# Both feed-forward blocks of a fused two-block transformer kernel computed by Strassen's seven products instead of eight

## The chip, the cores and the metric

The kernel runs on one core of a Trainium2 chip. The metric is the device time of one launch in microseconds (us). A core has TensorE (PE in the profile, PEld for its weight loads), VectorE (DVE), ScalarE (ACT), GpSimd (POOL) and SyncE (SP, which issues most of the transfers).

## The reference, cut to what matters

One sequence of 1024 tokens with 1024 features goes through a first transformer block (a SwiGLU feed-forward block, a token mixer, a second feed-forward block) and then through a two-layer second model. The change is in the two feed-forward blocks (FFN) of the first block:

```
def rms_norm(x, g):
    xf = x.astype(jnp.float32)
    y = xf * lax.rsqrt(jnp.mean(xf * xf, axis=-1, keepdims=True) + RMS_EPS)
    return (y * g.astype(jnp.float32)).astype(x.dtype)

def swiglu(x, w_gate, w_up, w_down):
    return (jax.nn.silu(x @ w_gate) * (x @ w_up)) @ w_down
...
        f1 = swiglu(rms_norm(x, ffn1_pre_g[l]), ffn1_w_gate[l], ffn1_w_up[l], ffn1_w_down[l])
        x = x + FFN_RESIDUAL_WEIGHT * rms_norm(f1, ffn1_post_g[l])
        m = token_mixer(rms_norm(x, mix_pre_g[l]), ...)
        x = x + rms_norm(m, mix_post_g[l])
        f2 = swiglu(rms_norm(x, ffn2_pre_g[l]), ffn2_w_gate[l], ffn2_w_up[l], ffn2_w_down[l])
        x = x + FFN_RESIDUAL_WEIGHT * rms_norm(f2, ffn2_post_g[l])
```

w_gate and w_up are 1024 x 2816, w_down is 2816 x 1024, all float32.

## The kernel before, in words

Everything is kept feature-major: 128 features on the partitions, tokens along the row, in two halves of 512 tokens (`HALVES`, c = 0 and 1). A float32 product is made of three matmuls in fp32r: each operand is split into a high part (a ScalarE copy) and a low part (value minus high part), and `pe_product` adds high x high (L401), weight low x high (L402) and weight high x low (L403), for each 128-row piece k.

Weights come in units of 128x1024 (512 KB), in the order of the list `UNITS`. SyncE loads them into two `raw` tiles, `act_units` makes `whi` (L366), `pool_units` makes `wlo` on GpSimd (L375), in a ring of three. One FFN has 22 column tiles j of 128 columns. For each j and each half c TensorE makes a gate product and an up product, 8 pieces k x 3 = 24 matmuls of 512 columns each, so 96 matmuls for a j. VectorE scales both by the norm's factor (`dve_scaled`, L794), ScalarE takes silu (L775), VectorE multiplies (L820), ScalarE and GpSimd make the high and the low part `hh`, `hl` (L781, L845). These stay in SBUF in a ring of four j. After every two j the down product of that pair is added: 8 feature tiles x 2 halves, each 2 pieces x 3 = 6 matmuls, and VectorE adds the PSUM result to `acc` (L831). That makes 22 x 96 + 11 x 96 = 3168 matmuls in each FFN.

Each engine runs its own list in program order, and semaphores order them against each other; there is no scheduler. `ffn_places` interleaves the work of j and of the down products on ScalarE, VectorE and GpSimd. Before an FFN stand the norms n1 (FFN 1) and n3 (FFN 2), behind it n2 and n4. Those behind it start during the last down products: the last pair's down products go through all eight tiles of half 0 first and then those of half 1, and beside the first four of half 1 TensorE sums the squares of half 0 (`after.beside`, L566), VectorE makes the root (`dve_variance` L590, `dve_root` L611 to L616), and `dve_apply` (L633, L638) begins when the last product is in.

Of the kernel before, what the change touches and what calls it, by code (L numbers as in the profile page):

```python
# [27 lines left out]
def _units():  # L28
    out = []

    def ffn(f):
        for b in range(11):
            out.extend([f"G{f}.{2 * b}", f"U{f}.{2 * b}"])
            if b:
                out.extend([f"D{f}.{b - 1}.0", f"D{f}.{b - 1}.1"])
            out.extend([f"G{f}.{2 * b + 1}", f"U{f}.{2 * b + 1}"])
        out.extend([f"D{f}.10.0", f"D{f}.10.1"])

    ffn(1)
# [4382 lines left out]
```

## Time and profile before

| what | value |
| --- | --- |
| three runs | 4032.33, 4038.79 and 4038.66 us, median 4038.66 us |
| span of the profiled execution | 4037.5 us (nothing beside its span is recorded) |
| TensorE busy | 3909.1 us, 97% |
| VectorE, ScalarE, GpSimd busy | 1910.4 us (47%), 1388.5 us (34%), 1425.1 us (35%) |
| share of the chain that ended last | PE 79%, DVE 12%, ACT 4%, POOL 3% |
| transfers | 206.07 MB, mean 51 GB/s |

Busy time of an engine is the union of its instructions' times. The matmuls of a group overlap each other, so a group's sum of durations is more than the time that it takes. FFN 1 lies at about 15 to 766 us of the span and FFN 2 at about 1550 to 2295 us.

### The profile page before, as it was taken

How to read it: one execution, taken by the hardware profiler on the slowest of the kernel's cores; microseconds unless marked ns; L12 is line 12 of the kernel's file. 1: busy time of each engine (PE TensorE's matmuls, PEld its weight loads, DVE VectorE, ACT ScalarE, POOL GpSimd, SP SyncE). 2: the span in 40 equal slices, each digit the busy share in tenths (PEclk: the TensorE clock that was granted, in tenths of full speed). 3: DMA queues.
4: the chain of work that ended last, by engine and by line, in shares of the span. 5: the costliest groups of instructions: out<-in, count | busy, mean ns of one | idle time of the engine just before them, and what ended most of it. 6: DMA issues, size and time to landing. Idle time of an engine off the chain costs nothing.

```text
span 4037.5 us, 49424 instructions
## 1 busy us (share of the span) xinstructions
PE 3909.1 (97%) x20636; PEld 3176.7 (79%) x20636; DVE 1910.4 (47%) x2824; ACT 1388.5 (34%) x2239; POOL 1425.1 (35%) x858
## 2 busy tenths in 40 slices
PE   8999999999999899999999999999999999999998
PEld 6888888666665467888888789999968998888877
DVE  3323222644355626323232477654377436666664
ACT  3111111322222234111111354331283336666663
POOL 2322323233543452223222224432271233434364
PEclk9999999999999999999999999999999999999989
DMA  2111111110000021111111101121112210000014
GB/s 95 52 42 53 44 51 51 55 58 22 27 22 16 16 95 53 53 47 47 47 51 44 42 27 43 53 95 54 64 50 74 106 58 24 27 29 29 24 64 139
DMA packets 57854, 206.07 MB, mean 51 GB/s; under 512 B 7392, under 2 KB 11008, under 8 KB 57248
## 3 DMA queue, kind: packets, MB, share of 16 engines
q1 hardware_dynamic: 45744, 158.55, 11.9%
q0 software_dynamic: 9328, 41.75, 2.8%
q8 instruction: 163, 2.67, 0.3%
q10 hardware_dynamic: 2560, 2.61, 0.2%
q14 instruction: 59, 0.48, 0.0%
HBM read 177.40 MB, written 25.49 MB: 50 GB/s over the span
## 4 chain that ended last, share of the span: by engine, by line
PE 79%; DVE 12%; ACT 4%; POOL 3%; issue 1%; DMA 0%; ACTq 0%; DVEq 0%; POOLq 0%
PE ps L401 16%; PE ps L403 15%; PE ps L402 15%; PE ps L3674 4%; PE ps L3606 2%; PE ps L3608 2%; PE ps L3607 2%; PE ps L1419 2%; POOL wlo L375 2%; PE ps L1421 2%; PE ps L1420 2%; PE ps L3658 2%; PE ps L3704 2%; PE ps L566 2%; PE ps L1538 2%; PE ps L1496 1%
## 5 line engine op out<-in xcount | busy, mean ns | idle before, releaser
L375 POOL TENSOR_TENSOR wlo<-raw,whi 128x1024 fp32r<-128x1024 f32 x286 | 692.5, 2431 | 799.7 <-ACT whi L366 799.6
L401 PE MATMUL ps<-fxh,whi 128*128 128x512 f32 x1488 | 602.7, 405 | 33.0 <-DVE fxl L653 17.3
L402 PE MATMUL ps<-fxh,wlo 128*128 128x512 f32 x1488 | 580.2, 390 | 0.0
L403 PE MATMUL ps<-fxl,whi 128*128 128x512 f32 x1488 | 580.1, 390 | 0.0
L401 PE MATMUL ps<-xh,whi 128*128 128x352 f32 (+1 forms) x1400 | 473.4, 338 | 6.3 <-DVE xl L653 2.7
L366 ACT ACTIVATE whi<-raw 128x1024 fp32r<-128x1024 f32 x286 | 294.8, 1049 | 455.5 <-PE ps L403 390.2
L402 PE MATMUL ps<-xh,wlo 128*128 128x352 f32 (+1 forms) x1400 | 450.5, 322 | 0.0
L403 PE MATMUL ps<-xl,whi 128*128 128x352 f32 (+1 forms) x1400 | 450.0, 321 | 0.0
L845 POOL TENSOR_TENSOR hl<-t,hh 128x512 fp32r<-128x512 f32 x88 | 114.1, 1296 | 722.7 <-ACT hh L781 722.7
L401 PEld LDWEIGHTS ps<-fxh,whi 128*128 128x128 f32 x1488 | 280.1, 188 | 111.2 <-issue 30.0
L402 PEld LDWEIGHTS ps<-fxh,wlo 128*128 128x128 f32 x1488 | 280.0, 188 | 67.4 <-issue 11.9
L403 PEld LDWEIGHTS ps<-fxl,whi 128*128 128x128 f32 x1488 | 279.9, 188 | 58.7
L3979 POOL TENSOR_TENSOR ospl<-osp,osph 128x672 fp32r<-128x672 f32 (+4 forms) x144 | 191.1, 1327 | 357.8 <-ACT osph L3800 356.8
L831 DVE TENSOR_TENSOR acc<-acc,ps 128x512 f32<-128x512 f32 x320 | 219.9, 688 | 205.0 <-PE ps L403 205.0
L401 PEld LDWEIGHTS ps<-xh,whi 128*128 128x128 f32 x1400 | 265.2, 189 | 17.8 <-issue 5.9
L401 PE MATMUL ps<-hh,whi 128*128 128x512 f32 x704 | 276.8, 393 | 1.2 <-POOL wlo L375 1.2
L403 PE MATMUL ps<-hl,whi 128*128 128x512 f32 x704 | 274.0, 389 | 0.0
L402 PE MATMUL ps<-hh,wlo 128*128 128x512 f32 x704 | 273.9, 389 | 0.0
L402 PEld LDWEIGHTS ps<-xh,wlo 128*128 128x128 f32 x1400 | 264.5, 189 | 8.1 <-issue 2.4
L403 PEld LDWEIGHTS ps<-xl,whi 128*128 128x128 f32 x1400 | 264.1, 189 | 0.0
L794 DVE TENSOR_TENSOR t<-ps,rs 128x512 f32<-128x512 f32 x88 | 60.6, 691 | 389.8 <-PE ps L403 389.8
L781 ACT ACTIVATE hh<-t 128x512 fp32r<-128x512 f32 x88 | 55.6, 632 | 497.2 <-DVE t L820 497.2
(431 smaller groups left out, 7771.7 us busy)
## 6 DMA issues: line engine op xcount, KB each, us to landing
raw<-in_w_dram SPq DMA_DIRECT2D x286, 512.0 KB, 3.3
rs_scratch<-res POOLq DMA_DIRECT2D x2, 4160.0 KB, 15.2
res<-rs_scratch POOLq DMA_DIRECT2D x8, 520.0 KB, 5.1
szin<-zs_scratch SPq DMA_DIRECT2D x8, 520.0 KB, 3.3
gs_scratch<-oot POOLq DMA_DIRECT2D x8, 520.0 KB, 5.7
res<-rs_scratch POOLq DMA_DIRECT2D x2, 1408.0 KB, 7.5
og<-gs_scratch POOLq DMA_DIRECT2D x16, 176.0 KB, 2.6
oot<-rs_scratch POOLq DMA_DIRECT2D x4, 704.0 KB, 5.5
```

The lines of the kernel that those rows point to most:

```text
L366: act.x.activation(K.whi[n % 3][:, :], K.raw[n % 2][:, :], ACT.Copy).then_inc(*S.up("w_hi", n))
L375: pool.x.tensor_tensor(K.wlo[n % 3][:, :], K.raw[n % 2][:, :], K.whi[n % 3][:, :], ALU.subtract).then_inc(*S.up("w_lo", n))
L401: pe.x.matmul(out, wh, xh, start=k == 0, stop=False)
L402: pe.x.matmul(out, wl, xh, start=False, stop=False)
L403: last = pe.x.matmul(out, wh, xl, start=False, stop=k == K - 1)
L566: pe.x.matmul(K.bank(b, n), K.m("ones"), square_tile(K, L, first)[:, 0:n], start=begin, stop=k == 7, skip_group_check=True).then_inc(*S.up ...
L831: dve.x.tensor_tensor(acc, acc, pp, ALU.add).then_inc(*S.up("dve_acc", (f, b, ft, c)))
L845: pool.x.tensor_tensor(K.hl[:, s, c0:c1], K.t[2 * c + 1][:, :], K.hh[:, s, c0:c1], ALU.subtract).then_inc(*S.up("pool_ffn", (f, j, c)))
L1419: pe.x.matmul(K.bank(b), a, x, start=k == 0, stop=False)
L1420: pe.x.matmul(K.bank(b), b_, x, start=False, stop=False)
L3674: last = pe.x.matmul(PS[:, (4 + i) * 512 + x0:(4 + i) * 512 + x1], mat[:, :], part[n % 2][:, i, 0:x1 - x0], start=first, stop=False, skip_ ...
L3979: pool.x.tensor_tensor(K.ospl[n % 2][:, :, 0:x1 - x0], K.osp[n % 2][:, :, 0:x1 - x0], K.osph[n % 2][:, :, 0:x1 - x0], ALU.subtract).then_i ...
```

## The change

Both FFNs work on a list of steps (`STEPS`), one step being a 128x512 weight operand (256 KB) that TensorE uses for 12 matmuls of 512 columns. For j = 0 and 1 the products stay as they were ("std", 4 steps for a j, each used twice as often). For j = 2 to 21 the gate and up products of both halves are a 2x2 block product (gate and up x lower and upper 512 features x two token halves), made by Strassen's algorithm in Winograd's form: seven steps M1, M5, M6, M3, M7, M2, M4 in place of eight. The down product is made at the end, in four blocks of 3, 3, 3 and 2 pairs of 128-row pieces, again seven products for eight: 77 steps. An FFN then has 2 x 96 + 20 x 84 + 77 x 12 = 2796 matmuls.

Strassen's products need sums. Sums of weights: four of the seven weight operands (M5, M6, M3, M7), on VectorE in the gate part and on GpSimd in the down part (`raw_sum`). Sums of token rows of the gate part: made once in each FFN by VectorE (`dve_mix`), beside the std products. Sums of rows of the down part: on VectorE (`dve_row_sum`), 4 of 7 steps. Sums of products: in PSUM, where later products go on in the bank of earlier ones, and in copies on ScalarE and reads on VectorE between them (`beside`); in the down part VectorE adds 28 tiles for each block to `acc` (`total`). The silu products are written to DRAM scratch `hs` and read back as rows of the down part, and their high and low parts are made again for each step (`act_row`, `dve_row_low`). The norm tiles of n1 and n3 have places of their own, rs1 is one tile of 512 columns, and the squares of the norm behind an FFN stand in the last step of all (`after.beside(p)` for p = 0 to 3).

```
+ORDER = ("M1", "M5", "M6", "M3", "M7", "M2", "M4")
+BLOCKS = ((0, 3), (3, 6), (6, 9), (9, 11))
...
+def pool_operand(pool, f, n):
...
+    pool.wait_ge("fw_hi", (f, n))
+    pool.x.tensor_tensor(lo, raw_tile(K, step, RAW_OF[step[2]]), hi, ALU.subtract).then_inc(*S.up("fw_lo", (f, n)))
...
+def pair_bank(p, m):
+
+    return 3 * p + {"M1": 0, "M6": 0, "M7": 0, "M4": 0, "M5": 1, "M3": 1, "M2": 2}[m]
...
+    def gate(n):
+        _, j, m = STEPS[n]
+        b = pair_bank(j % 2, m)
+        wh, wl = operand(n)
+        pe.bank(b)
...
+    act_operand(act, f, 4)
+    act_operand(act, f, 5)
+    std(0, 0)
+    act_mix(act, f, (0, 0))
+    act_operand(act, f, 6)
+    act_operand(act, f, 7)
+    std(0, 1)
+    act_mix(act, f, (0, 1))
...
+    std(1, 1)
+    act_mix(act, f, (1, 1))
+    late_done(act, norms)
+    for n in range(FIRST_GATE, NSTEP):
+        act_operand(act, f, n + 4)
+        before = STEPS[n - 1]
+        if before[0] == "gate":
+            beside(before[1], before[2])
+        act_row(act, f, n + 3)
...
+    std(0, 0)
+    dve_mix(dve, f, (0, 0), pre)
+    std(0, 1)
+    dve_mix(dve, f, (0, 1), pre)
+    raw_sum(dve, f, 9)
+    std(1, 0)
+    late_done(dve, norms)
+    dve_mix(dve, f, (1, 0), pre)
+    raw_sum(dve, f, 10)
+    raw_sum(dve, f, 11)
+    std(1, 1)
+    raw_sum(dve, f, 12)
+    dve_mix(dve, f, (1, 1), pre)
+    for n in range(FIRST_GATE, NSTEP):
+        before = STEPS[n - 1]
+        if before[0] == "gate":
+            beside(before[1], before[2])
+        if n + 5 < FIRST_DOWN:
+            raw_sum(dve, f, n + 5)
+        if STEPS[n][0] == "down":
+            totals(n)
+        dve_row_low(dve, f, n + 3)
+        dve_row_sum(dve, f, n + 4)
...
+    for n in range(FIRST_GATE, NSTEP):
+        pool_operand(pool, f, n + 4)
+        if FIRST_DOWN <= n + 5 < NSTEP:
+            raw_sum(pool, f, n + 5)
```

A step's `act_operand` waits until the step six before it is used up, its `act_row` until the one four before it is. TensorE's M6 goes on in M1's PSUM bank, so it waits until ScalarE has copied M1 out of it (`u1`, L998).

The first place where the order matters is ScalarE's list in FFN 1, around the passage from j = 0 and 1 to the rest. Before, with j = 1 here as one of many (whi is the high part of a weight unit, t_76 and t_78 take silu):

```order
L366 ACTIVATE whi_58<-raw_56 128x1024
L775 ACTIVATE t_76<-t_76 128x512
L781 ACTIVATE hh<-t_77 128x512
L775 ACTIVATE t_78<-t_78 128x512
L781 ACTIVATE hh<-t_79 128x512
```

Of the change (fwh is a step's high part, u_100 takes silu of j = 1, L983 makes the high parts of the mixed rows of M4, and L998 copies M1's bank):

```order
L811 ACTIVATE fwh_77<-fpa 128x512
L811 ACTIVATE fwh_78<-fpa 128x512
L992 ACTIVATE u_100<-u_100 128x512
L983 ACTIVATE fxh<-fyl 128x512 x4
L811 ACTIVATE fwh_73<-fpa 128x512
L811 ACTIVATE fwh_74<-fpa 128x512
L998 ACTIVATE u_94<-ps 128x512
```

The copy out of M1's bank now stands behind four high parts of rows that VectorE makes in its last piece of `dve_mix`.

VectorE's list ahead of those four is this, from the scaling of j = 1's half 1 (L1053, L1055, L1117) on; the L1081 to L1087 rows are one of the four mixed rows of M4, and three more follow with the low part (L1097) of each:

```order
L1053 TENSOR_TENSOR u_100<-ps,rs_69 128x512
L1055 TENSOR_TENSOR u_101<-ps,rs_69 128x512
L1117 TENSOR_TENSOR u_101<-u_101,u_100 128x512
L792 TENSOR_TENSOR fpa<-fpa 128x512
L1081 TENSOR_TENSOR fyh<-res 128x512
L1083 TENSOR_TENSOR fyl<-res 128x512
L1084 TENSOR_SCALAR fyl<-fyl,vec 128x512
L1087 SCALAR_TENSOR_TENSOR fyl<-fyh,vec,fyl 128x512
```

None of these rows was there before except the first three, which had another form.

The second place is GpSimd's list. Before, in the steady part of an FFN (hl is the low part of a silu product, wlo that of a weight unit):

```order
L845 TENSOR_TENSOR hl<-t_77,hh 128x512
L845 TENSOR_TENSOR hl<-t_79,hh 128x512
L375 TENSOR_TENSOR wlo_63<-raw_57,whi_60 128x1024
L375 TENSOR_TENSOR wlo_61<-raw_56,whi_58 128x1024
```

Of the change, in the down part (L820 makes a step's low part, L792 the sum of weights of the step behind it):

```order
L820 TENSOR_TENSOR fwl_82<-fpb,fwh_76 128x512
L792 TENSOR_TENSOR fpb<-fpb,u_96 128x512
L820 TENSOR_TENSOR fwl_83<-fpb,fwh_77 128x512
L792 TENSOR_TENSOR u_94<-u_94,u_97 128x512
L820 TENSOR_TENSOR fwl_84<-u_94,fwh_78 128x512
L792 TENSOR_TENSOR u_95<-u_95,u_98 128x512
L820 TENSOR_TENSOR fwl_79<-u_95,fwh_73 128x512
```

Low parts and sums alternate, and between a sum and the low part that uses it lies ScalarE's high part of that sum. This holds for the 12 steps of M5, M6, M3 and M7 of a block of three; the other nine have a low part alone.

## Rows read from the trace of the kernel before

**Rows 1.** The page: span and busy times of the engines.

```profile
span 4037.5 us, 49424 instructions
PE 3909.1 (97%) x20636; PEld 3176.7 (79%) x20636; DVE 1910.4 (47%) x2824; ACT 1388.5 (34%) x2239; POOL 1425.1 (35%) x858
```

**Rows 2.** The page's groups: sum of durations, mean ns of one, idle before.

```profile
L401 PE MATMUL ps<-fxh,whi 128*128 128x512 f32 x1488 | 602.7, 405 | 33.0 <-DVE fxl L653 17.3
L401 PE MATMUL ps<-hh,whi 128*128 128x512 f32 x704 | 276.8, 393 | 1.2 <-POOL wlo L375 1.2
```

**Rows 3.** Timeline of PE in FFN 1: start, us, instruction.

```profile
239.64 0.39 PE L401 MATMUL ps<-hh,whi 128*128 128x512 f32 x1
239.87 0.39 PE L402 MATMUL ps<-hh,wlo 128*128 128x512 f32 x1
...
252.34 0.39 PE L403 MATMUL ps<-hl,whi 128*128 128x512 f32 x1
```

**Rows 4.** Waits of PE, from 55 to 766 us and from 1600 to 2300 us.

```profile
PE ps L401 <- POOL wlo L375: 7.2, 12, 0.9
...
PE ps L401 <- POOL wlo L375: 6.8, 11, 0.9
```

**Rows 5.** Groups of VectorE by form: busy us, mean ns of one, idle before.

```profile
L831 DVE TENSOR_TENSOR acc<-acc,ps 128x512 f32<-128x512 f32 x320 | 219.9, 688 | 205.0 <-PE ps L403 205.0
L820 DVE TENSOR_TENSOR t<-t,t 128x512 f32<-128x512 f32 x88 | 61.9, 703 | 9.6 <-DVE t L794 0.9
L2320 DVE TENSOR_SCALAR scv<-sxin,vec 128x1040 f32<-128x1040 f32 x12 | 9.7, 806 | 0.1
```

**Rows 6.** Groups of ScalarE and GpSimd by form, 0 to 820 us.

```profile
L781 ACT ACTIVATE hh<-t 128x512 fp32r<-128x512 f32 x44 | 27.8, 632 | 248.6 <-DVE t L820 248.6
...
L845 POOL TENSOR_TENSOR hl<-t,hh 128x512 fp32r<-128x512 f32 x44 | 57.1, 1297 | 361.3 <-ACT hh L781 361.3
```

**Rows 7.** Timeline behind FFN 1, GpSimd's rows, then VectorE's rows.

```profile
742.94 4.76 POOL L375 TENSOR_TENSOR wlo<-raw,whi 128x1024 fp32r<-128x1024 f32 x2
764.21 2.98 POOL L581 TENSOR_TENSOR t<-t,t 128x512 f32<-128x512 f32 x2 [8.18 <-ACT t L546]
...
744.83 0.69 DVE L831 TENSOR_TENSOR acc<-acc,ps 128x512 f32<-128x512 f32 x1 [0.67 <-PE ps L403]
764.37 1.68 DVE L611 TENSOR_TENSOR t<-t,t 128x512 f32<-128x512 f32 x1
766.08 1.65 DVE L613 SCALAR_TENSOR_TENSOR t<-t,t 128x512 f32<-128x512 f32 x1
768.37 1.28 DVE L831 TENSOR_TENSOR acc<-acc,ps 128x512 f32<-128x512 f32 x2
```

**Rows 8.** Timeline at the start of FFN 1, VectorE and ScalarE.

```profile
49.51 0.69 DVE L590 TENSOR_SCALAR t<-ps 128x512 f32<-128x512 f32 x1 [4.29 <-PE ps L566]
77.38 0.42 DVE L794 TENSOR_TENSOR t<-ps,rs1a 128x256 f32<-128x256 f32 x1 [4.68 <-PE ps L403]
...
53.45 1.28 ACT L775 ACT_TABLE_LOAD   x1
```

**Rows 9.** Timeline at the end of FFN 1 and of FFN 2.

```profile
766.28 2.08 PE L566 MATMUL ps<-t,mat 128*128 128x512 f32 x4
...
769.57 0.94 DVE L633 SCALAR_TENSOR_TENSOR acc<-acc,vec,t 128x512 f32<-128x512 f32 x1
...
2295.06 4.89 PE L566 MATMUL ps<-lq,mat 128*128 128x352 f32 x16
...
2295.86 0.56 DVE L633 SCALAR_TENSOR_TENSOR acc<-acc,vec,t 128x336 f32<-128x336 f32 x1
```

**Rows 10.** Windows: busy PE, PEld, DVE, ACT, POOL, then clock, DMA share, GB/s.

```profile
776.00:780.00 4.00, 3.02 (x6) 1.46 (x5) 3.96 (x7) 2.46 (x4) 0.00 (x0) 0.52 0.20 81
780.00:784.00 4.00, 4.00 (x10) 2.27 (x9) 3.93 (x7) 3.04 (x6) 0.00 (x0) 0.62 0.00 0
```

**Rows 11.** Transfers by line (KB each, us to landing), and a window at the start.

```profile
raw<-in_w_dram SPq DMA_DIRECT2D x286, 512.0 KB, 3.3
...
12.00:16.00 4.00, 1.27 (x3) 0.83 (x3) 1.79 (x2) 3.52 (x8) 4.00 (x2) 1.00 1.04 394
```

More of the change, by code:

```diff
@@ L29, in _units @@
     out = []
[L31 to L39, printed above, removed]
     out.append("IN.24")
@@ new lines, in _ffn_steps @@
+def _ffn_steps():
+    out = []
+    for j in range(STD):
+        out.extend(("std", j, q) for q in ("A11", "A12", "A21", "A22"))
+    for j in range(STD, 22):
+        out.extend(("gate", j, m) for m in ORDER)
+    for b, (k0, k1) in enumerate(BLOCKS):
+        for m in ORDER:
+            out.extend(("down", b, m, k) for k in range(k1 - k0))
+    return out
+STEPS = _ffn_steps()
+STEP_AT = {s: n for n, s in enumerate(STEPS)}
+NSTEP = len(STEPS)
+FIRST_GATE = 4 * STD
+FIRST_DOWN = FIRST_GATE + 7 * (22 - STD)
@@ new lines, in down @@
+    def down(n):
+        _, b, m, k = STEPS[n]
+        end = k == BLOCKS[b][1] - BLOCKS[b][0] - 1
+        wh, wl = operand(n)
+        pe.wait_ge("ft_lo", (f, n))
+        xh, xl = row_ring(K, n)
+        for p in range(4):
+            o, pb = 128 * p, (0 if m in ("M1", "M6", "M7", "M4") else 4) + p
+            if k == 0:
+                pe.bank(pb)
+            pe.x.matmul(K.bank(pb), wh[:, o:o + 128], xh, start=m in FRESH and k == 0, stop=False, skip_group_check=True)
+            pe.x.matmul(K.bank(pb), wl[:, o:o + 128], xh, start=False, stop=False, skip_group_check=True)
+            last = pe.x.matmul(K.bank(pb), wh[:, o:o + 128], xl, start=False, stop=end, skip_group_check=True)
+            if p == 3:
+                last.then_inc(*S.up("pe_step", (f, n)))
+            elif end:
+                last.then_inc(*S.up("pe_step", (f, n, p)))
+            if end:
+                pe.banks[pb] = [("dve_acc", (f, b, m, p))]
+            if n == NSTEP - 1:
+                after.beside(p)
+        S.steps[f, n] = "pe_step", (f, n)
@@ L783, in act_ffn, with std, copied @@
-    ffn_places(act, f, gate_up, lambda b, c, ft: None, act_units, after)
+    def std(j, c):
+        ea = K.u[4 * (j % 2) + 2 * c][:, :]
+        act.wait_ge("dve_fe", (f, j, "gs", c))
+        act.x.activation(ea, ea, ACT.Silu).then_inc(*S.up("act_fe", (f, j, "silu", c)))
+    def copied(j, m, what, tile, free):
+        for name, key in free:
+            act.wait_ge(name, key)
+        act.wait_ge("pe_step", (f, STEP_AT["gate", j, m]))
+        act.x.activation(tile, K.bank(pair_bank(j % 2, m)), ACT.Copy).then_inc(*S.up("act_fe", (f, j, what)))
@@ L786, in dve_scaled @@
+    after.end()
 def dve_scaled(dve, f, j, c, norms):
     S, K = dve.S, dve.K
[L790 to L795 removed]
+    tile = (K.rs0, K.rs1)[c][:, :]
     b = 2 * ((2 * j + c) % 2)
+    u = 4 * (j % 2) + 2 * c
@@ new lines, in dve_ffn @@
+    dve_mix(dve, f, (1, 1), pre)
[9 more added lines that the diff above has]
+        dve_row_sum(dve, f, n + 4)
+    for p in range(4):
+        total(len(BLOCKS) - 1, "M4", p)
+        if p == 1:
+            after.beside(3)
+    after.beside(5)
```

599 lines of the change are left out of this document (447 added, 152 removed).

## The prediction

> **What bounds the kernel now.** I read the page first, then TensorE's timeline inside an FFN, then who waits for whom, then the timelines of the other engines at the start and the end of an FFN. The page shows TensorE busy for 97% of the span [rows 1]: what is taken from it shortens the kernel, unless another engine is then late. How much one matmul is worth is not in the page's groups. They give a mean of 393 to 405 ns [rows 2], but matmuls overlap: in the timeline the first and the last row are 56 matmuls apart and 12.70 us [rows 3], so one costs **0.2268 us** of TensorE, and a step of twelve 2.72 us. Inside the FFNs TensorE waits only for GpSimd's `wlo`, 7.2 and 6.8 us in all [rows 4].
>
> The Trainium skill says the same of such durations (Perfetto Trace Analysis, Identifying the Most-Contended Engine: matmul busy time is no good measure, since matmuls are pipelined). By the groups' mean the saving below would be 744 x 0.393 = 292 us, by the spacing it is 169 us.
>
> **What the change takes away.** Each FFN has 3168 - 2796 = 372 matmuls less, so 744 x 0.2268 = **168.7 us** less. The weights of a step are ready up to four or five steps ahead, so the 14.0 us of waits [rows 4] should go too. Bytes hardly matter: 512 KB land in 3.3 us and the engines moved 394 GB/s at their busiest [rows 11]; a gate tile asks for 1.5 MB in 19 us (79 GB/s), a down block for 6 MB in 57 us (105 GB/s), each asked for at least four steps ahead.
>
> **What it adds: prices.** A VectorE instruction of 512 columns with one input in PSUM takes 0.69 us, with both in SBUF 0.69 us when nothing disturbs it [rows 5]; back to back they start 0.61 us apart (the pair of 1.28 us in [rows 7]), 0.73 us apart where one needs the other's result. A tensor_scalar from SBUF is not there at 512 columns; at 1040 it takes 0.81 us [rows 5], so between 0.4 us (half of that) and 0.69 us: I take 0.57 us with the wait. ScalarE takes 0.63 us, GpSimd 1.30 us [rows 6].
>
> VectorE and GpSimd disturb each other. L831, with PSUM as one input, takes 0.69 us in the middle of GpSimd's 4.76 us [rows 7]. L611 and L613, with both inputs in SBUF, take 1.68 and 1.65 us beside GpSimd's pair, whose 2.98 us are 0.4 us over two times 1.28 us. So such instructions take turns: a GpSimd one and a VectorE one need 1.70 us together, and the one that is late waits for the other's end.
>
> **Start of an FFN.** This is the largest cost. VectorE's list, from the variance of half 1's norm (49.51 us [rows 8]) on:
> - variance, ScalarE's root, three VectorE steps, then silu's table load of 1.28 us [rows 8] and the first product: 6.9 us;
> - mixed rows of M5 and M6 for two k: 2 x (0.73 + 0.57 + 0.67 + 0.61 + 0.61) = 6.4 us, twice in the list: 12.8 us;
> - mixed rows of M7: 4 x (0.57 + 0.67 + 0.61) = 7.4 us;
> - three rounds of scaling and multiplying, 1.9 us each: 5.7 us; four weight sums: 2.4 us;
> - mixed rows of M4 up to the last one: 4 x (0.61 + 0.73 + 0.57 + 0.67) + 3 x 0.61 = 12.2 us;
> - collisions with GpSimd's eight low parts: bounds 0 and 8 x 1.1 us, I take 4 us.
>
> Sum 51.4 us. Then ScalarE makes the last high part, two operands and the copy of M1's bank (ScalarE's list): 2.3 us. So M6 can begin 53.7 us after 49.51 us. TensorE, which had its last std product read at 77.38 us [rows 8], 27.9 us after, does M1 and M5 in 5.4 us more and is ready for M6 at 33.3 us. It stands for **20.4 us**, part of it earlier (u of j = 1 waits some 4 us for its operands, which stand behind `act_mix`). Behind it the clock is low: after a TensorE idle for 2 to 4 us, 776 to 784 us has a granted clock of 0.52 and 0.62 of 2.4 GHz, its lower level 1.2 GHz [rows 10], which costs 8 x 0.43 = 3.4 us. Together 24 us for each FFN. Bounds: 14 us (tensor_scalar 0.4 us, no collisions) to 30 us. FFN 2 has the same lists. The first x tiles also share the queues with 1 MB more of weights (2.6 us at 394 GB/s [rows 11]); I take 1.5 us, and 0.5 us at FFN 2.
>
> **Gate steps.** Per j of 19.04 us: GpSimd 7 x 1.28 = 9.0 us; VectorE 13 instructions = 8.2 us, nine of them with two SBUF inputs; ScalarE 12 x 0.6 = 7 us. Work is four steps (10.9 us) ahead; the blocking costs a VectorE instruction at most 1.1 us. I take nothing. Without that cover each step would cost some 1 us.
>
> **Down steps.** In the twelve steps of M5 to M7 GpSimd needs a low part and a sum with ScalarE's high part between them: 1.28 + 1.28 + 0.63 + 0.15 for the hand-overs = 3.34 us, plus one VectorE turn of 0.43 us: 3.8 us against 2.72 us. It falls behind by 12 x 1.08 = 13 us and has 11 us in hand (operand n+5 is ready 2.6 us into step n); in the other nine steps it wins back 9 x 1.0. So 2 us in the first block, 5 in the next two, some 1 in the last: 13 us. At each of three block boundaries M1 starts in the banks that M4 has just left; the totals of p = 2 and 3 stand on VectorE behind a row's low part and sum, which wait for ScalarE: 0.75 + 3 x 0.61 + 0.4 = 3.0 us into a step, needed at 1.36 us: 1.6 us each, partly in the same time as the waits above. Together **16 us** an FFN; bounds 5 us (no turns of VectorE) and 60 us (below). The passage from gate to down adds 2 us: VectorE waits in `dve_row_low` for rows asked for when M3 ends (3.3 us and more to land) before it reads M7's bank for M4.
>
> **End of an FFN.** The squares of half 0 now stand in the last step, and root and last totals come behind them: variance 0.7, totals 1.2, root 2.2 us, so `dve_apply` starts 4.3 us after TensorE's last product and not 3.3 and 0.8 us after [rows 9]. With a collision, 1.5 and 4 us: 3 us each.
>
> **Sum.** -168.7 - 14.0 + 2 x (24 + 16 + 2 + 3) + 2.0 = -90.7 us. Against the profiled span of 4037.5 us that gives 3946.8 us; the median of the runs is 1.2 us over that span: **3948 us**.
>
> **Rivals.**
> - *VectorE and GpSimd bind the down part.* Port turns in a block of 21 steps: 33 GpSimd instructions x 1.28 + 33 of VectorE with two SBUF inputs x 0.55 = 60.4 us, and with twelve gaps of 0.78 us for ScalarE 69.8 us, against 57.1 us. Without any work in hand that is 3.32 us a step, 154 x 0.6 = 92 us in place of 32: 4008 us. For it: GpSimd is busy for 3/4 of the time. Against it: nine of 21 steps are light. The Trainium skill has the rule (SBUF — State Buffer, Who interferes with whom): a VectorE instruction with two SBUF inputs and a GpSimd one that reads SBUF exclude each other for a whole instruction. Rows 7 agree. Chance 0.18.
> - *Slower.* The same place, but VectorE too always comes second: 1.57 instructions x 1.70 + totals 1.33 x 0.61 = 3.5 us, and hand-overs make it 3.9 us a step. 154 x 1.18 = 182 us in place of 32: 4098 us. It decides from a down step of 3.52 us on (32 + 90.7 = 122.7 us over 154 steps, 0.80 us each). Chance 0.10.
> - *Nearly all of it is kept.* VectorE's start is hidden (tensor_scalar short, operands in time) and the buffers carry the down part: -182.7 + about 40 = 3896 us. Against it: VectorE's sum of 51 us has only a few free terms. Chance 0.12.
> - *A matmul is worth its duration* (292 us, 3750 us or less): rows 3 speak against it. Chance 0.01.
>
> **How the numbers follow.** The forecast (3915 to 3985 us) has 0.59. The range from 3890 to 4025 us leaves out the slower rival and the tails, some 0.17. A difference under 0.2% (8 us) can't be told from none. Faster 0.88 (the forecast, the first rival but for 0.02, the third and fourth), same 0.02, slower 0.10.
>
> **What would show it.** TensorE's matmuls in FFN 1 still 0.227 us apart; a wait of 15 to 18 us at M6 of j = 2 in both FFNs, ended by ScalarE's copy of M1's bank; GpSimd over 70% busy in the down part, VectorE's SBUF instructions there over 0.9 us in the mean while the totals stay at 0.69 us; waits of TensorE for `fwl` in M3 and M7 of the blocks. A down part of over 3.3 us a step would make the forecast wrong, as would gate steps that are not 2.72 us long.

## The result, and the profile of the changed kernel

The changed kernel takes **3996.01 us** (median of four runs, 3995.18 to 4000.23) against 4038.72 us before: a ratio of 0.9898 with a 95% interval from 0.9884 to 0.9912. It is 43 us faster where 91 us were forecast. The time lies in the range, but the gain is less than half of the forecast one: 48 us were missing, and 3996 us is nearer to the first rival (4008 us) than to the forecast (3948 us).

The first line of the page gives the span, the second busy times and counts, to be read beside [rows 1]:

```profile
span 3993.3 us, 50138 instructions
PE 3769.9 (94%) x19892; PEld 3051.9 (76%) x19892; DVE 2422.4 (61%) x3232; ACT 1640.2 (41%) x2775; POOL 1788.9 (45%) x1176
```

TensorE has its 744 matmuls less, and its share fell from 97 to 94%: it waits more. For whom it waits is told by its list of waits (engine, tile and line; whom it waited for; us in all, times, the longest):

```profile
PE ps L954 <- DVE acc L1167: 30.3, 10, 7.6
PE ps L936 <- ACT u L998: 28.5, 2, 14.8
...
PE ps L954 <- DVE acc L1161: 14.1, 6, 5.7
PE ps L954 <- DVE u L1122: 12.3, 2, 6.4
...
PE ps L418 <- DVE u L1055: 7.5, 2, 3.7
...
PE ps L954 <- DVE fxl L863: 2.4, 8, 0.7
...
PE ps L954 <- POOL fwl L820: 1.4, 2, 0.7
```

The second and the fifth row are the start of the two FFNs, as forecast. L954 is the down part. There TensorE hardly waits for the low parts of weights (`fwl`, 1.4 us), which were to be its main wait. It waits 44.4 us for VectorE's totals, L1167 and L1161, and 12.3 us at the passage for the last read of the gate part (L1122).

No matmul record is missing in the FFNs, so the start times of every twelfth matmul give the length of each step. Less the 2.72 us of [rows 3] that is each step's excess. It is 0.1 us or less in all gate steps of FFN 1 but three. In the down part of FFN 1, worked out from the trace (one number per step; a wait at the start of a step counts for the step before it):

```
block 0  18.7  M1 7.29 1.84 0   M5 0 0 0   M6 0 0 0   M3 0.18 1.01 0.96   M7 1.05 0.43 0.08   M2 0 0 0   M4 0 0 5.85
block 1   9.8  M1 2.38 0.01 0   M5 0 0 0   M6 0 0 0   M3 0 0 0            M7 1.04 0.43 0.08   M2 0 0 0   M4 0 0 5.84
block 2  12.7  M1 3.61 0.69 0   M5 0 0 0   M6 0 0 0   M3 0 0 0            M7 0.18 0.43 0.12   M2 0 0 0   M4 0 0 7.73
block 3   9.6  M1 3.61 1.52     M5 0 0     M6 0 0     M3 0 0              M7 0 0              M2 0 0     M4 0 4.47
```

The 4.47 us at the end hold the eight squares of the norm. The 9.1 us in M1 of block 0 belong to the passage from gate to down. Nearly all else stands where M4 hands its banks to M1 of the next block. This is the first of these places, rows of GpSimd, ScalarE, VectorE and TensorE by time (start, duration, instruction, idle time before it and what ended it):

```profile
544.74 1.77 DVE L840 TENSOR_TENSOR fyh<-fyh 128x512 f32<-128x512 f32 x1
546.60 0.63 ACT L854 ACTIVATE fxh<-fyh 128x512 fp32r<-128x512 f32 x1 [2.34 <-PE ps L956]
547.14 0.61 ACT L811 ACTIVATE fwh<-fpb 128x512 fp32r<-128x512 f32 x1
547.83 3.08 POOL L820 TENSOR_TENSOR fwl<-fpb,fwh 128x512 fp32r<-128x512 f32 x2 [1.87 <-ACT fwh L811]
...
550.88 1.81 POOL L792 TENSOR_TENSOR fpb<-fpb,u 128x512 f32<-128x512 f32 x1
...
552.72 0.63 ACT L811 ACTIVATE fwh<-fpb 128x512 fp32r<-128x512 f32 x1 [3.40 <-POOL fpb L792]
553.25 0.61 ACT L854 ACTIVATE fxh<-fyl 128x512 fp32r<-128x512 f32 x1
...
553.90 1.34 DVE L863 TENSOR_TENSOR fxl<-fyl,fxh 128x512 fp32r<-128x512 f32 x1 [2.35 <-ACT fxh L854]
...
555.16 1.74 DVE L840 TENSOR_TENSOR fyl<-fyl 128x512 f32<-128x512 f32 x1
...
556.83 1.27 DVE L1161 COPY acc<-ps 128x512 f32<-128x512 f32 x2
...
557.65 0.76 PE L954 MATMUL ps<-fxh,fwh 128*128 128x512 f32 x1 [5.69 <-DVE acc L1161]
```

M4's banks are full at 551.96 us. VectorE is idle at that time, but the read of the banks (556.83) stands in its list behind a row's low part (553.90) and the next sum of rows (555.16). The low part waits for ScalarE's high part (553.25), which is queued behind the weight's (552.72), and this one waits for GpSimd's sum (550.88). So a wait named after VectorE's totals may be GpSimd's lateness, come to light in a list that is worked off in order. Whether it is the order or the lateness can't be read from one trace.

Two rows of windows show the clock behind a stall (columns: the window, us, busy time with count of PE, PEld, DVE, ACT, POOL, then clock, DMA share, GB/s). After 5.7 us of idleness it is 0.68 of full speed in the mean from 558 to 562 us, between its two levels of 1.2 and 2.4 GHz, then full:

```profile
558.00:562.00 4.00, 3.29 (x9) 2.07 (x9) 3.80 (x5) 0.63 (x1) 3.26 (x3) 0.68 0.81 299
562.00:568.00 6.00, 6.00 (x28) 4.94 (x28) 3.62 (x4) 2.42 (x4) 4.40 (x5) 1.00 0.01 3
```

### The profile page after: what moved, and what is told of

Same layout as the page of the kernel before. It is cut to its first block, busy times and chain, and to the rows that moved or that the text cites. A ratio compares the mean times of both kernels' runs of the same rounds, so it can differ in the third digit from the quotient of the medians.

```text
span 3993.3 us, 50138 instructions
## 1 busy us (share of the span) xinstructions
PE 3769.9 (94%) x19892; PEld 3051.9 (76%) x19892; DVE 2422.4 (61%) x3232; ACT 1640.2 (41%) x2775; POOL 1788.9 (45%) x1176
## 3 DMA queue, kind: packets, MB, share of 16 engines
q1 hardware_dynamic: 90096, 204.71, 15.2%
## 4 chain that ended last, share of the span: by engine, by line
PE 69%; DVE 17%; POOL 5%; ACT 5%; issue 3%; DMA 1%; SPq 0%; ACTq 0%; DVEq 0%; POOLq 0%
PE ps L936 6%; PE ps L937 6%; PE ps L938 6%; PE ps L418 5%; PE ps L419 5%; PE ps L420 5%; PE ps L4143 4%; PE ps L4075 2%; PE ps L4077 2%; PE ps L4076 2%; PE ps L1886 2%; PE ps L1888 2%; PE ps L1887 2%; PE ps L4127 2%; POOL fwl L820 2%
## 5 line engine op out<-in xcount | busy, mean ns | idle before, releaser
L392 POOL TENSOR_TENSOR wlo<-raw,whi 128x1024 fp32r<-128x1024 f32 x154 | 377.0, 2452 | 472.2 <-ACT whi L383 472.2
L418 PE MATMUL ps<-xh,whi 128*128 128x352 f32 (+1 forms) x1400 | 473.4, 338 | 6.1 <-DVE xl L674 2.7
L820 POOL TENSOR_TENSOR fwl<-fpa,fwh 128x512 fp32r<-128x512 f32 x184 | 261.4, 1432 | 285.4 <-ACT fwh L811 283.2
L820 POOL TENSOR_TENSOR fwl<-fpb,fwh 128x512 fp32r<-128x512 f32 x180 | 258.1, 1444 | 291.1 <-ACT fwh L811 288.9
L954 PE MATMUL ps<-fxh,fwh 128*128 128x512 f32 x616 | 255.5, 415 | 60.5 <-DVE acc L1167 30.3
L1122 DVE TENSOR_TENSOR u<-ps,u 128x512 f32<-128x512 f32 x120 | 82.6, 689 | 301.0 <-PE ps L938 301.0
L936 PE MATMUL ps<-fxh,fwh 128*128 128x512 f32 x640 | 249.1, 389 | 3.2 <-DVE u L1122 3.2
L938 PE MATMUL ps<-fxl,fwh 128*128 128x512 f32 x640 | 249.0, 389 | 0.0
L937 PE MATMUL ps<-fxh,fwl 128*128 128x512 f32 x640 | 249.0, 389 | 0.0
L955 PE MATMUL ps<-fxh,fwl 128*128 128x512 f32 x616 | 248.9, 404 | 0.0
L956 PE MATMUL ps<-fxl,fwh 128*128 128x512 f32 x616 | 248.2, 403 | 0.0
L936 PE MATMUL ps<-fth,fwh 128*128 128x512 f32 x480 | 188.7, 393 | 28.5 <-ACT u L998 28.5
L383 ACT ACTIVATE whi<-raw 128x1024 fp32r<-128x1024 f32 x154 | 160.7, 1050 | 124.9 <-DMA raw<-in_w_dram 51.7
L954 PEld LDWEIGHTS ps<-fxh,fwh 128*128 128x128 f32 x616 | 121.0, 196 | 102.0 <-issue 46.6
L4075 PE MATMUL ps<-xh,whi 128*128 128x352 f32 (+1 forms) x576 | 188.6, 328 | 3.7 <-DVE ovt L4334 3.3
L937 PE MATMUL ps<-fth,fwl 128*128 128x512 f32 x480 | 188.3, 392 | 0.0
```

Source lines behind the costliest of these rows:

```text
L392: pool.x.tensor_tensor(K.wlo[n % 3][:, :], K.raw[n % 2][:, :], K.whi[n % 3][:, :], ALU.subtract).then_inc(*S.up("w_lo", n))
L418: pe.x.matmul(out, wh, xh, start=k == 0, stop=False)
L820: pool.x.tensor_tensor(lo, raw_tile(K, step, RAW_OF[step[2]]), hi, ALU.subtract).then_inc(*S.up("fw_lo", (f, n)))
L936: pe.x.matmul(K.bank(b), wh[:, o:o + 128], xh, start=m in FRESH and i == 0, stop=False, skip_group_check=True)
L937: pe.x.matmul(K.bank(b), wl[:, o:o + 128], xh, start=False, stop=False, skip_group_check=True)
L938: last = pe.x.matmul(K.bank(b), wh[:, o:o + 128], xl, start=False, stop=i == 3, skip_group_check=True)
```

## The experiments

Each time is a median of four runs (seven in the last one); the kernel before had 4034 to 4039 us beside them. The last five columns are the excess in FFN 1 in us, as above: of all gate steps (with the wait at M6), and of each block of the down part.

Two theories stand against each other in the expectations. Theory A: the order of VectorE's list holds the banks. Theory B: the down part is bound by the making of operands, and the wait for the banks only shows it. B has two forms, B1 (the chain of sum, high part and low part on GpSimd and ScalarE is too long by itself) and B2 (instructions of GpSimd and of VectorE with both inputs in SBUF take turns, and the turns add up).

| run | time | ratio to before, 95% interval | gate | block 0 | 1 | 2 | 3 |
|---|---|---|---|---|---|---|---|
| changed kernel | 3996.0 | 0.9898, 0.9884 to 0.9912 | 18.1 | 18.7 | 9.8 | 12.7 | 9.6 |
| e1 banks | 3989.4 | 0.9885, 0.9871 to 0.9900 | 18.1 | 12.8 | 9.8 | 9.8 | 13.3 |
| e2 GpSimd's order | 3964.9 | 0.9827, 0.9811 to 0.9844 | 18.5 | 12.3 | 6.5 | 5.6 | 9.3 |
| e3 start | 3988.8 | 0.9884, 0.9870 to 0.9899 | 15.9 | 16.6 | 10.8 | 12.7 | 9.6 |
| e5 = e1 + e2 | 3950.7 | 0.9790, 0.9775 to 0.9805 | 18.9 | 8.1 | 4.0 | 4.5 | 8.6 |
| e6 = e1 + sums on VectorE | 3977.1 | 0.9854, 0.9839 to 0.9868 | 18.6 | 11.4 | 8.1 | 8.1 | 12.1 |
| e7 = e1, no sums of rows | 3948.3 | 0.9782, 0.9767 to 0.9797 | 17.3 | 12.5 | 3.9 | 3.9 | 5.3 |
| e8 = e3 + reads earlier | 3982.9 | 0.9871, 0.9854 to 0.9887 | 15.2 | 16.6 | 11.0 | 12.9 | 6.8 |
| e9 = e5 + e8 | 3941.2 | 0.9763, 0.9748 to 0.9778 | 12.7 | 8.8 | 4.7 | 4.7 | 9.7 |
| e10 = e6, two orders | 3921.4 | 0.9719, 0.9702 to 0.9737 | 18.3 | 6.1 | 0.1 | 0.1 | 7.5 |
| e11 = e10 + e8 | 3910.9 | 0.9697, 0.9681 to 0.9712 | 12.8 | 5.7 | 0.1 | 0.0 | 7.4 |
| e12 = e5, rows first | 3939.3 | 0.9760, 0.9744 to 0.9775 | 17.9 | 8.8 | 2.4 | 1.9 | 7.3 |
| e13 = e6, one order | 4049.0 | 1.0038, 1.0026 to 1.0049 | 18.0 | 19.1 | 18.4 | 17.3 | 18.7 |

**e1: other banks at a block's start.**

```diff
+def down_bank(b, m):
+    return 4 if (m in ("M1", "M6", "M7", "M4")) == (b % 2 == 0) else 0
...
-            o, pb = 128 * p, (0 if m in ("M1", "M6", "M7", "M4") else 4) + p
+            o, pb = 128 * p, down_bank(b, m) + p
```

> The sum was 48 us short, nearly all of it in the down parts: TensorE is 31.2 and 31.3 us late at the three block boundaries of each FFN and 10.6 and 11.1 us at the passage from gate to down, and each of these waits is for VectorE's read of a PSUM bank. Edit: the first product of a block uses the four banks that M4 of the block before did not use (blocks 0 and 2 begin in banks 4 to 7), so that no first product waits for the read of a bank just left. Theory A (order: VectorE's list puts the bank's read behind a row's low part and sum that wait for others, and TensorE waits for nothing else): the boundaries and the passage fall from 42 to under 8 us in each FFN, time 3996 - 2 x 34 = about 3930 us. Theory B, the first rival of the prediction (the chain of GpSimd's sums and low parts with ScalarE between them binds the down part at 3.3 us a step, the wait is only where it comes to light): the lag turns up as waits for fwl or fxl in M5 to M7 and in the first products, a block still takes 67 to 70 us, time 3985 to 3996 us. Between them the share of each can be read off: each us kept of the 84 is theory A's.

Theory B: the time lies in its range. The waits at the block boundaries are gone, and blocks 1 and 2 are still 66.9 us long (66.9 and 69.9 us before the edit). Their excess now stands in M5 to M7, with 1.0 us in nearly every step. TensorE still waits 10.0 us for totals in FFN 1's down part, but at other places than the boundaries, and 6.4 us of them in the last block. This is a step of M5 to M7 (the line numbers lie four higher than in the changed kernel):

```profile
638.95 1.75 POOL L796 TENSOR_TENSOR fpa<-frc,fpa 128x512 f32<-128x512 f32 x1
639.46 1.78 DVE L844 TENSOR_TENSOR fyh<-fyh 128x512 f32<-128x512 f32 x1
640.73 0.63 ACT L815 ACTIVATE fwh<-fpa 128x512 fp32r<-128x512 f32 x1 [2.49 <-POOL fpa L796]
641.33 0.63 ACT L858 ACTIVATE fxh<-fyh 128x512 fp32r<-128x512 f32 x1
641.43 1.29 POOL L824 TENSOR_TENSOR fwl<-fpa,fwh 128x512 fp32r<-128x512 f32 x1 [0.74 <-ACT fwh L815]
642.00 1.28 DVE L867 TENSOR_TENSOR fxl<-fyh,fxh 128x512 fp32r<-128x512 f32 x1 [0.76 <-ACT fxh L858]
642.69 1.73 POOL L796 TENSOR_TENSOR fpa<-frc 128x512 f32<-128x512 f32 x1
```

GpSimd's chain from sum to sum is 3.74 us: the sum 1.73 to 1.75 (1.28 and a turn of VectorE's), 0.74 for ScalarE and the hand-overs, the low part 1.29. The prediction had 3.8 us for it. VectorE's sum of rows, 0.69 us by itself, lasts 1.78 beside it.

**e2, e5: GpSimd's sum ahead of its low part**, alone and with e1's banks.

```diff
-        pool_operand(pool, f, n + 4)
         if FIRST_DOWN <= n + 5 < NSTEP:
             raw_sum(pool, f, n + 5)
+        pool_operand(pool, f, n + 4)
```

> Edit: in GpSimd's list of the down part the sum for step n+5 stands ahead of the low part for step n+4 instead of behind it, so that ScalarE makes the high part of a summed operand while GpSimd is busy with another low part (the gap of 0.8 us and ScalarE's 0.63 us between sum and low part go). Banks as in the changed kernel. Theory B (GpSimd's chain binds): a summed step falls from 3.7 to about 3.0 us, the waits at boundaries shrink, 12 x 0.7 = 8 us in each of eight blocks at most, time 3996 - 40 to 60 = 3936 to 3956 us. Theory A (VectorE's order binds): each boundary still waits for the row of step n+2 and its sum, but the row comes earlier by what ScalarE waited for the sum (2.4 us at each boundary), time 3996 - 6 x 2.4 = about 3982 us.

> Both edits of the down part together: the banks of the blocks alternate, and GpSimd's sum stands ahead of the low part. Theory A (order of bank reads) gives the same as the banks alone, about 3930 us. Theory B (GpSimd's chain) gives the same as the other order of GpSimd's list alone or a little less, 3936 to 3956 us. If both hold, each hides behind the other: either alone gives little and the two together bring the down part down to near 57.2 us a block, time 3996 - 2 x 45 = about 3906 us.

e2 gained 31 us and lies in neither theory's range, 9 us over B's and 17 us under A's. e5 gained 45 us, which is in B's range and half of the 90 us expected if both theories held. The banks are worth 7 us on the changed kernel and 14 us on top of e2: the order of the bank reads is a real cost, but a small one as long as GpSimd and VectorE are late anyway. In e5 GpSimd runs back to back and still needs about 3.5 us a summed step:

```profile
562.37 1.84 POOL L796 TENSOR_TENSOR u<-u,fpb 128x512 f32<-128x512 f32 x1
562.38 0.68 DVE L867 TENSOR_TENSOR fxl<-fyl,fxh 128x512 fp32r<-128x512 f32 x1
562.98 1.78 DVE L844 TENSOR_TENSOR fyl<-fyh,fyl 128x512 f32<-128x512 f32 x1
564.17 1.75 POOL L824 TENSOR_TENSOR fwl<-u,fwh 128x512 fp32r<-128x512 f32 x1
...
564.68 1.27 DVE L1171 TENSOR_TENSOR acc<-acc,ps 128x512 f32<-128x512 f32 x2
```

Each of these GpSimd instructions takes 1.28 us and another 0.47 to 0.56 us, the turn of a VectorE instruction with two SBUF inputs. VectorE's `L844` takes 1.78 us, which is the other side of the same turn. Its two totals (one input in PSUM) take 1.27 us for both, undisturbed beside GpSimd. The Trainium skill says that a VectorE instruction with two SBUF inputs contends with a GpSimd instruction that reads SBUF, and that one with at most one SBUF input, as the totals are, does not (SBUF — State Buffer, Who interferes with whom). These rows agree.

**e7: no sums of rows**, on e1's banks. `dve_row_sum` returns at once, and `act_row` waits for the transfer in the place of the sum. The kernel leaves this part of the computation out.

> Edit on top of the alternating banks (3989 us): VectorE makes no sums of rows in the down part (48 in each FFN, in the steps of M5, M6, M7 and M4; this part of the computation is left out, the rows of one quarter are used in the place of each sum). GpSimd's list is as before. Each such sum lasted 1.75 us beside GpSimd's work where an undisturbed one lasts 0.69. Theory B1 (GpSimd's chain of sum 1.28, ScalarE 0.63 with hand-overs 0.78, low part 1.28 binds by itself): 3.34 us a summed step remain, of the 1.0 us of excess 0.6 stay, time 3989 - 96 x 0.4 = about 3950 us. Theory B2 (turns with VectorE bind): the same 0.4 us go, and GpSimd's own sums become 1.28 us long; if also the hand-overs were lengthened by VectorE, below 3940 us. Rival (VectorE's row sums cost nothing, they run in VectorE's own time): 3985 us or more, steps stay at 3.7 us.

The time is B1's, but for another reason. The step with a sum of weights was still 3.74 us: with the sum of rows gone, GpSimd's sum shared a turn with VectorE's low part. What changed is that the blocks carry work ahead again: in blocks 1 and 2 M5 and M6 run without excess and only M3 and M7 show the 1.0 us. Block 0, which follows the gate part, gained nothing (12.5 against 12.8 us). So in the later blocks the sums of rows cost what the light steps were to win back. In M4's steps of the changed kernel VectorE's list of sum (1.77 us), totals (1.27 us) and low part (0.68 us) paces the whole chain: the sums start 3.5 us apart, where TensorE's step is 2.72 us (from the first row here to 544.74 us in the rows of the boundary):

```profile
541.24 1.77 DVE L840 TENSOR_TENSOR fyh<-fyh 128x512 f32<-128x512 f32 x1
542.94 1.27 DVE L1167 TENSOR_TENSOR acc<-acc,ps 128x512 f32<-128x512 f32 x2
543.11 0.63 ACT L854 ACTIVATE fxh<-fyh 128x512 fp32r<-128x512 f32 x1 [2.34 <-DVE fyh L840]
...
544.13 0.68 DVE L863 TENSOR_TENSOR fxl<-fyh,fxh 128x512 fp32r<-128x512 f32 x1
```

**e6: the weight sums on VectorE**, behind its sum of rows, on e1's banks: `raw_sum(dve, f, n + 5)` follows `dve_row_sum(dve, f, n + 4)`, and GpSimd's call goes.

> Edit on top of the alternating banks (3989 us): the weight sums of the down part are made by VectorE behind its sum of rows, as in the gate part, and no longer by GpSimd; the same sums, 96 of them. With the alternating banks a step of M5 to M7 took 3.7 us (1.0 us more than TensorE's 2.72), one of the others 2.72. Theory B1 (the chain on GpSimd alone binds: its sum, ScalarE's high part, its low part): GpSimd is left with one low part of 1.28 us a step and the excess goes, 4 blocks x 10 to 13 us x 2 FFNs = 80 to 90 us less, about 3910 us. Theory B2 (turns at the port: instructions of VectorE and of GpSimd with both inputs in SBUF exclude each other, and VectorE has totals besides): a step needs 1.28 us of GpSimd and 3 x 0.55 to 0.61 us of VectorE in turn, 2.9 to 3.1 us, and VectorE's totals (0.61 us, 1.33 a step) fit only in part beside GpSimd: 3.0 to 3.3 us a summed step, 96 x 0.3 to 0.6 us kept, 3935 to 3960 us. If VectorE, once loaded, is worse than GpSimd: above 3989 us.

It gained 12 us against e1, and lies 17 us over the upper end of theory B2's range; B1 was out by 67 us. With GpSimd down to one instruction a step, VectorE binds, and not by its own work alone:

```profile
565.48 0.68 DVE L844 TENSOR_TENSOR fyl<-fyh,fyl 128x512 f32<-128x512 f32 x1
566.08 0.68 DVE L796 TENSOR_TENSOR u<-u,fpb 128x512 f32<-128x512 f32 x1
566.68 1.27 DVE L1171 TENSOR_TENSOR acc<-acc,ps 128x512 f32<-128x512 f32 x2
...
567.50 1.29 POOL L824 TENSOR_TENSOR fwl<-u,fwh 128x512 fp32r<-128x512 f32 x1 [2.49 <-ACT fwh L815]
567.98 1.36 DVE L867 TENSOR_TENSOR fxl<-fyl,fxh 128x512 fp32r<-128x512 f32 x1
```

The low part of the rows (567.98) meets GpSimd's (567.50) and waits 0.8 us for its end, while the totals, which would not have to wait, are done already.

**e10, e13: who stands in whose turn.** e10 changes two orders of e6, e13 only the second:

```diff
 # ScalarE (e10 only)
+        if n >= FIRST_DOWN:
+            act_row(act, f, n + 3)
         act_operand(act, f, n + 4)
...
-        act_row(act, f, n + 3)
+        if n < FIRST_DOWN:
+            act_row(act, f, n + 3)
...
 # VectorE (e10 and e13)
+        dve_row_low(dve, f, n + 3)
         if STEPS[n][0] == "down":
             totals(n)
-        dve_row_low(dve, f, n + 3)
```

> Edit on top of VectorE making the down part's weight sums (3977 us): ScalarE makes the rows' high part ahead of the operand's, and VectorE makes the rows' low part ahead of the totals, so that the totals, which have an input in PSUM, stand where GpSimd's low part holds the turn. In the run before, VectorE's low part lasted 1.36 us (0.7 of it waiting for GpSimd's 1.28 us) and the summed step was 3.78 us: 1.36 + 0.60 + 0.60 + 1.21. Theory B2 (turns of SBUF-only instructions): 0.6 + 1.28 (totals beside it) + 0.6 + 0.6 = 3.1 us a summed step, 0.4 over TensorE instead of 0.75 to 1.1; with the work carried ahead from the light steps most blocks lose under 3 us: 3977 - 2 x 4 x 5 = about 3935 us, down to 3925 us. Theory B1 (no turns, only the length of each engine's own list): VectorE has the same instructions as before and the time stays at 3970 to 3980 us. Loss: the operand's high part now waits for the row's, GpSimd comes later, 3985 us.

> One of the two edits of the 3921 us run alone, to part them: on top of VectorE making the weight sums (3977 us), VectorE makes the rows' low part ahead of the totals; ScalarE still makes the operand's high part ahead of the row's. Theory B2 (turns): the operand's high part still lets GpSimd's low part begin before the row's high part is there, so VectorE's low part still waits for the end of GpSimd's 1.28 us, and now the totals, which used that time in part, stand behind it: no gain or a loss, 3970 to 3990 us; it takes both edits. Rival (VectorE's order alone did it, the totals held the rows back): near 3921 us, at most 3935 us.

e10 holds exactly the instructions of e6 and is 56 us faster, 4 us better than theory B2's lowest figure; B1 falls. Blocks 1 and 2 have no excess: they run at TensorE's 57.2 us. The transfers are those of e6 too, so they are not what made these blocks longer. The low part of the rows now runs ahead of GpSimd's, and the totals beside it:

```profile
560.81 0.69 DVE L867 TENSOR_TENSOR fxl<-fyl,fxh 128x512 fp32r<-128x512 f32 x1 [0.16 <-ACT fxh L858]
561.40 1.30 POOL L824 TENSOR_TENSOR fwl<-u,fwh 128x512 fp32r<-128x512 f32 x1 [1.90 <-ACT fwh L815]
561.42 1.28 DVE L1174 TENSOR_TENSOR acc<-acc,ps 128x512 f32<-128x512 f32 x2
562.62 0.69 DVE L844 TENSOR_TENSOR fyl<-fyl 128x512 f32<-128x512 f32 x1
563.22 0.68 DVE L796 TENSOR_TENSOR fpb<-u,fpb 128x512 f32<-128x512 f32 x1
```

From `L867` to the next `L867` (564.06 us) are 3.25 us, where e6 has 3.78. That is still more than TensorE's 2.72 us, and it is now made up for by the light steps.

VectorE's order alone (e13) is a loss of 72 us against e6. That this order alone does not bring the gain was right, the size was not (3970 to 3990 us expected). Whether it takes both is not shown: no run has ScalarE's order alone on top of e6, so how the 56 us divide stays open. The rows of e13 show what I had left out:

```profile
568.45 1.34 DVE L867 TENSOR_TENSOR fxl<-fyl,fxh 128x512 fp32r<-128x512 f32 x1 [1.22 <-ACT fxh L858]
569.71 1.27 DVE L1165 COPY acc<-ps 128x512 f32<-128x512 f32 x2
570.91 0.67 DVE L844 TENSOR_TENSOR fyl<-fyh,fyl 128x512 f32<-128x512 f32 x1
571.51 0.68 DVE L796 TENSOR_TENSOR fpb<-fpb 128x512 f32<-128x512 f32 x1
...
573.40 1.35 DVE L867 TENSOR_TENSOR fxl<-fyl,fxh 128x512 fp32r<-128x512 f32 x1 [1.22 <-ACT fxh L858]
```

The totals had also filled the 1.22 us in which VectorE waits for ScalarE's two high parts; now that time is idle in each such step and the totals come on top: 4.95 us for this one.

**e12: ScalarE's order alone, on e5.** The edit is e10's first hunk.

> Edit on top of the alternating banks with GpSimd's sums ahead of its low parts (3951 us, where GpSimd runs back to back with 1.75 us for each of its instructions, 1.28 without a turn of VectorE): ScalarE's rows ahead of its operands as in the two runs above. GpSimd and VectorE already fill their turns (2 x 1.28 + 2 x 0.47 = 3.5 us a summed step). Theory B2: the order of ScalarE's list changes nothing, 3946 to 3956 us. Theory B1 or A (somebody waits for ScalarE's order): more than 8 us either way.

Theory B2's range was wrong: 11 us faster, which is what I had put down for "somebody waits for ScalarE's order". In blocks 1 and 2 of FFN 1 the excess begins at M3 and no longer at M6, so these blocks carry more ahead. In FFN 2 it still begins at M6, and these blocks are 0.5 and 1.1 us shorter. The two down parts together are 7 us shorter; the rest of the 11 us is not assigned. A likely reason, which no run tests by itself, is that a row's high part no longer stands behind that of a weight whose sum is late. I had looked at the rate of the summed steps and not at the lead with which a block enters them.

**e3, e8: the start.** e3 puts the copies of the banks of M1, M5 and M6 of j = 2 and the operands 12 and 13 ahead of `act_mix(act, f, (1, 1))`; e8 also puts VectorE's reads of M3 (with its scaling) and M7 ahead of the last of M4's mixed rows.

> Edit at the start of each FFN: ScalarE copies the banks of M1, M5 and M6 of j = 2 and makes the high parts of two operands ahead of the four high parts of M4's mixed rows instead of behind them. TensorE stands there for 14.8 and 13.7 us at M6, waiting for the copy of M1's bank, while ScalarE's own first high part of M4 comes 5 us after its last work. Theory: nothing but the order of ScalarE's list holds M6; M6 and M3 (5.4 us) run in the time of the wait, M7 too if its operand is there, then TensorE waits at M7 or M2 for an operand or at M7 for VectorE's reads, which stand behind all of the mixed rows of M4. Gain 2 to 4 steps of 2.72 us less what the clock costs: 5 to 10 us an FFN, time 3976 to 3986 us. Rival: VectorE's list ends the stall whatever ScalarE does, since its own work for the mixed rows of M4 is not shortened and M4 waits for it: M6 to M2 are done early, the stall only moves to M4 and is as much shorter as these four steps last (10.9 us an FFN, 3975 us); if the copies delay ScalarE's high parts for M4, no gain or a loss.

> Edit at the start on top of the earlier ScalarE copies (3989 us alone), down part as in the changed kernel: VectorE reads the banks of M3 and M7 of j = 2 (C12, its scaling, C22) ahead of the last of M4's four mixed rows instead of behind all of them and two more instructions. With the copies alone the stall moved from M6 to M4, 7.9 us, and ended with the read of C22 at 110.34 us; M4's last low part had been done by 104.5 us. Theory: M4 can start at about 106.3 us (VectorE's list without the weight sum and the second scaling), 4 us an FFN less, 3981 us. Rival: GpSimd's and ScalarE's operands for M4 and the following M1, which stand behind the high parts of M4's mixed rows, are then late (low parts at 105.56 to 108.95 us), and nothing is gained: 3989 us.

The wait at M6 of 14.8 us became one of 7.9 us at M4 with e3. The profile names nobody for it, but VectorE's read of M7's bank (C22) ended at 110.34 us and M4 began at 110.44 us, so VectorE's list ends the stall, as the rival had it. 7 us came out, less than either theory's 10 to 21: M4 still waits for everything on VectorE's list ahead of that read. e8, which moves the read forward, gave 6 us more (3983 us, 3981 us expected) and a wait of 5.1 us at the same place, now for GpSimd's operand of M4:

```profile
PE ps L936 <- POOL fwl L820: 5.1, 1, 5.1
PE ps L936 <- ACT u L998: 4.4, 2, 2.6
```

**e9, e11: the combinations.**

> All edits together: alternating banks and GpSimd's sums ahead of the low parts (together 3951 us) with the two edits of the start (7 us and what the second one gives). The start and the down part are 380 us apart in each FFN, so the gains should add: 3951 - 7 - 0 to 8 = 3936 to 3944 us. If the gate part carries less work ahead into the passage (less slack on VectorE), up to 3950 us.

> The edits of the run above with the two of the start. The start gave 11 to 13 us of the changed kernel's time in its own run (3983 against 3996 us) and is 380 us away: the run above minus 10 to 13 us, 3915 to 3925 us if theory B2 holds there.

e9 came out in its range, e11 4 us below its own. Start and down part add for the most part: the edits of the start are worth 13 us on the changed kernel, 9.5 us on e5 and 10 us on e10. e11 is the fastest version, 3910.9 us, 3.0% under the kernel before and 85 us under the changed one.

## Why the prediction was right in part, and where it failed

The step that failed is the term for the down steps, 16 us an FFN: it measured 37 to 38 us. With it went the passage, 2 us, which measured 11 us. Against the 92 us of costs forecast (24 + 16 + 2 + 3 for each FFN, and 2 us) stand 138.5 us: 168.7 + 14.0 less the 44.2 us by which the profiled spans differ.

- **Matmuls, 168.7 us, and the gate steps at nothing: right.** 137 of 140 gate steps in each FFN have their 2.72 us within 0.1 us; the other three are the wait at M6, the step behind it and the passage.
- **Start of an FFN, 24 us: right.** FFN 1 has a wait of 3.7 us and 1.7 us of low clock at u of j = 1, and 16.7 us at M6: 22.2 us. FFN 2 has 22.9 us. The wait at M6 is ended by ScalarE's copy of M1's bank in both, 0.2 us short of the 15 to 18 us in FFN 1 (14.8) and 1.3 us short in FFN 2.
- **Passage, 2 us: wrong.** It is 10.6 and 11.1 us. VectorE's read of M4's bank (489.66 us) stood behind a row's low part, as I wrote of M7's bank; but the low part that counted waited, through ScalarE's list, for GpSimd's sum of a weight, and this for a transfer until 484.2 us. No run takes this place by itself; in e10 it is 6.3 and 7.6 us.
- **Down steps, 16 us: this step failed.** It is 37.2 us in FFN 1 and 37.8 us in FFN 2: the steps of M3 and M7 with 6.0 and 5.5 us, and the three block boundaries with 31.2 and 32.3 us (not the 31.3 us that e1's expectation gives for FFN 2), where I had 1.6 us each. Both sums lie within the bounds of 5 and 60 us that I had given. I had put only p = 2 and 3 behind a row and a sum of rows. The totals of p = 0 and 1 stand behind the same two, of steps n + 2 and n + 3, and these hang on GpSimd's sum for step n + 3. So the lag that I had looked for at `fwl` came to light there.
- **Why there was a lag at all:** the rate was right (3.8 us a summed step forecast, 3.74 measured), the account of the work ahead was not. I let the nine light steps of a block win back 1.0 us each, so that M5 starts with 11 us in hand. In e1 blocks 1 and 2 show the 1.0 us from the second step of M5 on, so they start with next to nothing in hand: M4's steps have sums of rows of their own, stretched from 0.69 to 1.77 us, and VectorE makes such a step in 3.5 us. e7 takes those sums away and six steps of M5 and M6 run free again.
- **The first rival's arithmetic was the better model.** It had 69.8 us a block without work in hand; blocks 1 and 2 took 66.9 to 69.9 us. The same sum follows some of the experiments: without the gaps for ScalarE 60.4 us (e5: 61.2 and 61.7), with the sums on VectorE 21 x 1.28 + 45 x 0.55 = 51.6 us, under TensorE's 57.2 us (e10: 57.3 and 57.2). It is no bound: e12, with e5's 60.4 us, took 59.0 and 59.6 us in FFN 1, and e6 (65.3 us) and e13 (74.4 and 75.6 us), with e10's 51.6 us, took far more, since the sum knows nothing of how the turns are placed. My reason against this rival, nine light steps, was the assumption that failed.
- **The signs.** The one that I had named against the forecast came: a down part of over 3.3 us a step. FFN 1's took 260.3 us for 77 steps, 3.38 us each with the passage's share and the squares. Of the others, the spacing held, GpSimd was busy for 70% of FFN 1's down part, and VectorE's low parts and sums of rows there took 1.20 us in the mean beside totals of 0.68 us. The waits for `fwl` did not come.
- **End, 3 us each: half right.** From an FFN's last product to the first product behind it TensorE needs 6.2 and 3.4 us more than before. `dve_apply` starts 7.1 and 4.6 us after the last product, where I had 4.3 us.
- **The first x tiles, 2 us in all:** the kernel's first product comes 3.0 us later (17.72 against 14.72 us).
- **Not in the sum:** outside of the FFNs some 6 us were gained that nothing in the prediction accounts for; no run looked into it.

The four parts of an FFN add up to 76 and 75 us. The two traces give 74 us from the span's start to the first product behind FFN 1 (757.50 against 775.46 us), and 71 us from FFN 2's first product to the first behind it; the difference is not assigned.

One sum puts the result in a plainer light. The down part of FFN 1 takes 260 us, from 481.83 to 742.1 us. Without Strassen's products it would be 88 steps, and at 2.72 us each these would take 239.5 us. In the changed kernel the whole gain is made by the gate part, and the down part gives some of it back; in e10 it takes 223 us.

## What to carry to other kernels

When work is moved from TensorE to VectorE and GpSimd, add up their instructions with two SBUF inputs as turns at one resource over a whole block, and count as time in hand only what the light steps leave after that sum. The sum says what is at stake, not what will come: the same 51.6 us a block went with 57.2, 65.3 and 75 us. Then place the instructions that read PSUM where the other engine holds the turn: the same instructions in another order were worth 56 us here, and one half of that change of order alone cost 72 us. A wait that names the read of a bank may be another engine's lateness, in a list that is worked off in order: give the bank an alternative, and see whether the time goes or only moves.
